# Expert weights loaded during the mixing stage, and the whole down product as rounded products, with ScalarE copying the result

## What is computed

```
x    = x + gt1 * rms_norm(mixed, g_post_mix)
hn2  = rms_norm(x, g_pre_ffn) * (1 + sc2) + sh2
group  = argmax(hn2 @ w_group_router + b_g)             # 4 groups
top 2 of the 4 experts of that group, weights from two softmaxes
act  = silu(hn2 @ w_gate[e]) * (hn2 @ w_up[e]) * weight # 16 experts, width 256
ffn  = sum over the two experts of act @ w_down[e]
x    = x + gt2 * rms_norm(ffn, g_post_ffn)
```

## Time and profile before

| | |
|---|---|
| median of three runs | 1550.93 us |
| the profiled execution, its own time | 1550.65 us |
| its span in the trace | 1548.8 us |
| TensorE busy | 1337.6 us, 86% |
| VectorE busy | 1140.9 us, 74% |
| ScalarE busy | 752.1 us, 49% |
| mixing ends, experts begin | at about 957 and 959 us of the span |
| loop: gate_up(2) begins, last down ends | at 1027 and 1481 us |
| bytes moved in the slice from 968 to 1007 us | 351 GB/s |

### The profile page before, as it was taken

The page is one execution under the profiler, slowest core; times in us unless marked ns, Lnnn a source line. Parts: engine busy times, 40 slices in busy tenths (PEclk is TensorE's granted clock), DMA queues, the critical chain, the costliest instruction groups (busy, mean ns, idle before and its releaser), DMA issues. The chain is left out here.

```text
span 1548.8 us, 24582 instructions
## 1 busy us (share of the span) xinstructions
PE 1337.6 (86%) x7046; PEld 1016.0 (66%) x7047; DVE 1140.9 (74%) x2094; ACT 752.1 (49%) x1614; POOL 538.8 (35%) x720
## 2 busy tenths in 40 slices
PE   5999999989997798699999994489999999999910
PEld 2688888856665465577777773267777777777700
DVE  3888888747675776366666664788989988988738
ACT  2423323213337477244444441167777777777633
POOL 1116776632226820012221122234443544444300
PEclk9999999979999999799999997699999999999965
DMA  9423444499867541333334433946798887884597
GB/s 335 131 94 133 180 157 156 153 341 342 291 209 209 165 138 58 132 136 136 135 135 161 157 129 127 351 133 158 195 267 239 252 240 191 267 222 107 129 327 287
DMA packets 138558, 298.30 MB, mean 193 GB/s; under 512 B 22228, under 2 KB 79829, under 8 KB 135998
## 3 DMA queue, kind: packets, MB, share of 16 engines
q1 hardware_dynamic: 110950, 219.74, 40.9%
q0 software_dynamic: 20800, 61.13, 17.0%
q10 hardware_dynamic: 6736, 16.55, 3.0%
HBM read 314.69 MB, written 102.25 MB: 269 GB/s over the span
## 5 line engine op out<-in xcount | busy, mean ns | idle before, releaser
L2683 DVE TENSOR_TENSOR ex_w_lo<-ex_wgu,ex_w_hi 128x1024 fp32r<-128x1024 f32 x192 | 226.1, 1220 | 47.6 <-ACT ex_w_hi L2480 46.9
L2480 ACT ACTIVATE ex_w_hi<-ex_wgu 128x1024 fp32r (+1 forms) x192 | 192.3, 1055 | 44.3 <-issue 31.0
L2443 POOL DMA_INDIRECT scratch_acc<-ex_o,ex_to x48 | 95.7, 1994 | 251.5 <-DVE ex_o L2713 170.7
L120 PE MATMUL ex_ps_h<-ex_w_hi,ex_xT 128*128 128x512 f32 x384 | 156.2, 407 | 3.4 <-DVE ex_x_lo L2677 3.4
L122 PE MATMUL ex_ps_h<-ex_w_hi,ex_x_lo 128*128 128x512 f32 x384 | 151.8, 395 | 0.0
L121 PE MATMUL ex_ps_h<-ex_w_lo,ex_xT 128*128 128x512 f32 x384 | 151.1, 393 | 0.0
L120 PE MATMUL fr_ps_m<-fr_whi,fr_hl 128*128 128x512 f32 (+1 forms) x384 | 138.7, 361 | 0.9 <-DVE fr_wlo L631 0.5
L122 PE MATMUL fr_ps_m<-fr_whi,fr_hl 128*128 128x512 f32 (+1 forms) x384 | 136.0, 354 | 0.0
L121 PE MATMUL fr_ps_m<-fr_wlo,fr_hl 128*128 128x512 f32 (+1 forms) x384 | 135.9, 354 | 0.0
L1941 POOL TENSOR_SCALAR mx_st<-mx_st 128x1 f32<-128x1 f32 x68 | 29.4, 433 | 268.1 <-ACT mx_j L1985 151.5
L120 PE MATMUL mx_ps_m<-mw_hi,mx_hT 128*128 128x512 f32 x272 | 107.9, 397 | 4.1 <-issue 2.1
(11 more groups left out here) (479 smaller groups left out, 3378.9 us busy)
## 6 DMA issues: line engine op xcount, KB each, us to landing
ex_wgu<-in_w_exp_gate_dram SPq DMA_DIRECT2D x51, 1024.0 KB, 11.8
ex_wgu<-in_w_exp_up_dram SPq DMA_DIRECT2D x51, 1024.0 KB, 14.1
ex_wd<-in_w_exp_down_dram SPq DMA_DIRECT2D x51, 1024.0 KB, 13.6
scratch_rec<-fr_w SPq DMA_DIRECT2D x16, 1112.0 KB, 4.2
s_rec<-scratch_rec SPq DMA_DIRECT2D x32, 556.0 KB, 5.8
scratch_proj<-fr_io SPq DMA_DIRECT2D x16, 640.0 KB, 3.0
scratch_acc<-in_zeros_dram SPq DMA_DIRECT2D x18, 512.0 KB, 5.7
scratch_x<-mx_x SPq DMA_DIRECT2D x17, 512.0 KB, 2.7
```

The costliest lines, as they stand in the source:

```text
L120: nc.tensor.matmul(out, hi, w_hi, start=first, stop=False)
L2443: pool.indirect_dma_start(T["acc"], bass.IndirectOffsetOnAxis(to[:, t:t + 1], 0), o[:, t % 2, :], None, compute_op=ALU.add).then_inc(sem(" ...
L2480: A(w_hi[:, par, c * PW:(c + 1) * PW], wgu[:, bass.ds(slot * (KD * 2 * DE) + c * PW, PW)], ACT.Copy).then_inc(S["w_rounded"], 1)
L2683: vec.tensor_tensor(w_lo[:, par, c * PW:(c + 1) * PW], wgu[:, bass.ds(slot * (KD * 2 * DE) + c * PW, PW)], w_hi[:, par, c * PW:(c + 1) * P ...
```

## The change

1. A new class `Routing` holds buffers that lie where the mixing weights lay. SP loads the constants at the start of mixing, and as soon as the last output product is done (`mix_done`) it issues the six loads of the first experts' gate and up weights, inside mixing. Tile 16's two stores go to ScalarE's queue. `square_mix` of tile 16 moves ahead of `move` of tile 15.
2. At the entry of `moe` the waits for the constants go. SP issues `w5` at once. TensorE's product with it comes before the sort products. VectorE takes the first part of `split_w(0)` ahead of `cmp`, the rest and the modulation row later. SP counts up the semaphores of the first three tiles itself, so ScalarE's `round_w(1)` and `round_w(2)` wait for the plan and the loads and not for SP.
3. AHEAD becomes 3: SP's order is `gate_up_weights(t+3)`, then `down_weights(t)`.
4. The second 128 rows of the down product become three rounded products too. `round_d` and `split_d` do both halves of the weights and of `a`. VectorE's `out` goes; ScalarE copies both halves of the result. TensorE's register reads go.
5. NKEPT becomes 1, so 16 tiles of `x2` are loaded at the end instead of 14.

```diff
+    def load_first(self, sp, T):
+        slots = self.wgu[:, :].rearrange("p (s k f) -> p s k f", s=NSL, k=KD)
+        for e in range(NSL):
+            for half, name in enumerate(("w_exp_gate", "w_exp_up")):
+                view = T[name].rearrange("a e (k p) f -> p (a e) k f", p=P)
+                sp.dma_start(slots[:, e, :, half * DE:(half + 1) * DE], view[:, e, :, :]).then_inc(self.first_gu[e], 16)
...
-            store(Tile(0, LAST))
-            sp.wait_ge(S["kept"], 32)
+            sp.wait_ge(S["mix_done"], NT)
+            plan.load_first(sp, T)
+            sp.wait_ge(S["kept"], 64)
...
                 if after:
                     glu(after)
+                else:
+                    square_mix(tile)
...
-            square_mix(Tile(0, LAST))
             square_x2(Tile(0, LAST))
+            end = Tile(0, LAST)
+            act.wait_ge(S["hn_ready"], NT)
+            act.dma_start(hnv[:, LAST:LAST + 1, :], hn[:, end.par, :].unsqueeze(1)).then_inc(end.sem("sth"), 16)
+            act.dma_start(x2v[:, LAST:LAST + 1, :], x[:, end.par, :].unsqueeze(1)).then_inc(end.sem("stx"), 16)
...
-NKEPT = 3
+NKEPT = 1
 LAG = 3
-AHEAD = 2
+AHEAD = NSL
...
+            for n in range(NSL):
+                sp.sem_inc(S["gu", n], 32)
+                sp.sem_inc(S["d", n], 16)
...
-            for t in range(AHEAD):
-                gate_up_weights(t, t)
+            for t in range(U):
+                gate_up_weights(t + AHEAD, (t + AHEAD) % U)
+                if t >= NSL:
+                    down_weights(t, t)
+            store_row5()
...
-            with sp.Fori(0, NTILE // U - 1) as i:
+            with sp.Fori(1, NTILE // U - 1) as i:
                 for n in range(U):
                     gate_up_weights(i * U + n + AHEAD, (n + AHEAD) % U)
                     down_weights(i * U + n, n)
...
-                A(a_hi[:, :], ps_a[:, 0:P], ACT.Copy, scale=0.5).then_inc(S["a_moved"], 1)
-                A(aT[:, 1, :], ps_a[:, P:2 * P], ACT.Copy, scale=0.5).then_inc(S["a_moved"], 1)
+                A(a_hi[:, :, :], ps_a[:, 0:2 * P].rearrange("p (k n) -> p k n", k=2), ACT.Copy, scale=0.5).then_inc(S["a_moved"], 1)
...
-                A(wd_hi[:, :], wd[:, bass.ds(slot * (2 * D), D)], ACT.Copy).then_inc(S["d_rounded"], 1)
+                for k in range(2):
+                    A(wd_hi[:, k, :], wd[:, bass.ds(slot * (2 * D) + k * D, D)], ACT.Copy).then_inc(S["d_rounded"], 1)
...
-                A(o[:, par, 0:512], ps_o[:, 0:512], ACT.Copy).then_inc(S["o_out_a"], 1)
+                for c in range(2):
+                    A(o[:, par, c * 512:(c + 1) * 512], ps_o[:, c * 512:(c + 1) * 512], ACT.Copy).then_inc(S["o_out_a"], 1)
...
-                vec.tensor_tensor(wd_lo[:, :], wd[:, bass.ds(slot * (2 * D), D)], wd_hi[:, :].bitcast(F32), ALU.subtract).then_inc(S["d_split"], 1)
+                for k in range(2):
+                    dve.wait_ge(S["d_rounded"], t * 2 + k + 1)
+                    vec.tensor_tensor(wd_lo[:, k, :], wd[:, bass.ds(slot * (2 * D) + k * D, D)], wd_hi[:, k, :].bitcast(F32), ALU.subtract).then_inc(S["d_split"], 1)
...
-                    three_products(nc, ps_o[:, at], a_hi[:, :], a_lo[:, :], wd_hi[:, at], wd_lo[:, at], True, False)
-                    last = nc.tensor.matmul(ps_o[:, at], aT[:, 1, :], wd[:, bass.ds((slot * 2 + 1) * D + c * 512, 512)], start=False, stop=True)
+                    pe.wait_ge(S["o_out_a"], t * 2 + c + 1)
+                    for k in range(2):
+                        last = three_products(nc, ps_o[:, at], a_hi[:, k, :], a_lo[:, k, :], wd_hi[:, k, at], wd_lo[:, k, at], k == 0, k == 1)
```

More of the change, by code:

```diff
@@ L1804, with mixing @@
 GELU_C = 2.0 * math.sqrt(2.0 / math.pi) / 2.0
-def mixing(nc, T, top, m, lg):
+def mixing(nc, T, top, m, lg, plan):
     with Stage(nc, top, "mx") as s:
@@ L1915, in _ @@
             clear(NT)
+            sp.dma_start(plan.rc[:, :], T["rconst"]).then_inc(S["kept"], 16)
+            sp.dma_start(plan.before[:, :], T["before"]).then_inc(S["kept"], 16)
             for b in range(2):
@@ L2651, in _, with split_w @@
                 dve.wait_ge(S["matched"], n + 1)
+            def split_w(t, par, parts, slot):
+                for c in parts:
+                    dve.wait_ge(S["w_rounded"], t * PARTS + c + 1)
+                    vec.tensor_tensor(w_lo[:, par, c * PW:(c + 1) * PW], wgu[:, bass.ds(slot * (KD * 2 * DE) + c * PW, PW)],
+                                      w_hi[:, par, c * PW:(c + 1) * PW].bitcast(F32), ALU.subtract).then_inc(S["w_split"], 1)
+            split_w(0, 0, range(1), 0)
             tt(cmp[:, :, :], C["tau"][0:1, :].unsqueeze(2).broadcast_to([1, NTILE, NE]), end[0:1, :].unsqueeze(1).broadcast_to([1, NTILE, NE]), ALU.is_ge)
@@ L2728, in step @@
                     split_w(t + 2, par, range(PARTS // 2), slot)
-                out(t - 1, 1 - par, i * (U // 2) + (k - 1) // 2)
                 split_d(t, own)
@@ L2769, in _ @@
             nc.tensor.matmul(ps_c, ones_h[:, :], a16, start=True, stop=True).then_inc(S["counted"], 1)
+            pe.wait_ge(S["w5_in"], 3 * 16)
+            for k in range(KD):
+                for j in range(4):
+                    last = nc.tensor.matmul(ps_h[32 * j:32 * j + 32, 1, 0:256], c5[:, k, :], w5(k)[:, j * 256:(j + 1) * 256], start=(k == 0), stop=(k == KD - 1))
+            last.then_inc(S["mm5"], 1)
             for n in range(2):
@@ L2774, in _ @@
             last.then_inc(S["turned"], 1)
-            pe.wait_ge(S["w5_in"], 3 * 16)
-            for k in range(KD):
-                for j in range(4):
-                    last = nc.tensor.matmul(ps_h[32 * j:32 * j + 32, 0, 0:256], c5[:, k, :], w5(k)[:, j * 256:(j + 1) * 256], start=(k == 0), stop=(k == KD - 1))
-            last.then_inc(S["mm5"], 1)
             def flip_x(t, n, q, first=False):
@@ L2867, in hybrid_layer @@
     early = Semaphores(nc)
-    with Stage(nc, None, "kept") as kept:
+    with Semaphores(nc) as top, Stage(nc, None, "kept") as kept, Stage(nc, top, "route") as route:
         lg = kept.sb("lg", [P, NT, NR])
@@ L2876, in hybrid_layer @@
             with Stage(nc, late, "mw") as weights:
-                mw = MixingWeights(weights)
+                plan = Routing(route)
+                mw = MixingWeights(weights, plan)
                 attention(nc, T, late, mw, first, early)
-                mixing(nc, T, late, mw, lg)
-        with Semaphores(nc) as top:
-            moe(nc, T, top, lg)
+                plan.constants(route)
+                mixing(nc, T, late, mw, lg, plan)
+        moe(nc, T, top, lg, plan)
 INS = ["x_prompt", "x_sample", "cache_k", "cache_v", "state_ssm_re", "state_ssm_im", "c_prompt", "c_sample",
```

144 lines of the change are left out of this document (68 added, 76 removed).

## The result

| | before | after |
|---|---|---|
| median of six runs beside each other | 1552.03 us (1549.96 to 1556.07) | 1557.85 us (1555.91 to 1559.91) |
| profiled execution, its own time | 1550.65 us | 1556.37 us |
| span of that execution | 1548.8 us | 1554.5 us |
| last logits of the mixing stage | 957.20 us | 952.05 us |
| `flip_x(3)` to the last `flip_x`, 44 periods | 426.94 us | 439.28 us |

The ratio is 1.0031, with a 95% interval of 1.0017 to 1.0045. The changed kernel is slower, by 5 to 6 us: more than the measurement is uncertain, less than the 0.5% that the forecast took as its bound for a difference. The forecast was 1550.

What follows compares the result with a forecast made beforehand. TensorE, busy 420 of 420 us, bounds the loop, VectorE close behind; nothing is full at the entry. 1550.65 - 9.9 (entry) + 6.5 (loop: -15.5 + 15 + 7) + 2.5 (end) = 1549.75, forecast 1550, range 1536 to 1564.

Steps and rivals of the forecast that it cites:

- TensorE's share: Loop: three rounded matmuls replace the float32 pair, saving 0.35 us a tile, 15.5 us in 44, if TensorE never waits.
- The register read: Loop: ScalarE's slow read before `round_w`, formerly hidden by slack, now comes through in part: +15 us, between 11 and 22.
- Rival (a): Loop: the engines keep up, reads hidden and down loads in time, TensorE sets 9.35: 1528 us, chance 0.12.
- AHEAD and the down weights: Loop: down loads behind fresh pairs land 1 to 2.5 us late in six tiles: +7 us, bounds 0 to 15.
- Rival (c): Loop: the clock falls in the stalls of the six late loads, 14 us on top: 1564 us, chance 0.13.
- The entry: From tile 16's `square_mix` to `gate_up(2)`: earlier work and fewer waits give -9.9 us, bounds -6 and -12.
- The barrier: Entry: SP, blocked issuing six megabytes until about 956.5, holds the barrier 1.5 us past the logits: +1.5 us.
- The end: After the loop: two more loads of 0.5 MB stand before the last scatter: +2.5 us, between 0 and 3.
- Kept at nothing: Semaphores, the constants' early loads in mixing and TensorE's dropped reads were given no cost or gain.
- (b): Loop: only one cost bites; reads without late loads 1543 us, loads without reads 1536 to 1541; chance 0.18.
- (d): Loads land at 17 us or more, or the entry gives only 6: +8 to +10, 1558 to 1562 us, chance 0.15.
- a period of 9.35: Loop, a sign of being right: TensorE's period without waits falls from 9.7 to 9.35 us.

Runs made afterwards that it cites:

- e5: Kernel of e1 with the old down product put back (second half one full float32 product, VectorE and ScalarE sharing the result copy): 1548.62 us, ratio 0.9980.
- e1: Changed kernel with each step issuing the down weights of tile t+1, not t, behind the gate and up weights of tile t+3: 1539.52 us, ratio 0.9921.
- e4: Kernel of e1 with GpSimd's next gather moved ahead of its three small operations, those one tile further on: 1537.88 us, ratio 0.9904.
- e3: Kernel before with only its constant AHEAD at 3 in place of 2: 1564.52 us, ratio 1.0084.
- e10: Kernel of e1 with 4 MB, not 6, of early expert weights, the third pair following the modulation weights after the barrier: 1543.66 us, ratio 0.9944.
- e8: Kernel of e1 with GpSimd's scatter of each tile also waiting for the next tile's second rounded down weights: 1549.24 us, ratio 0.9994.
- e7: Kernel of e1 with the places of `ex_w_hi` and `ex_w_lo` in memory exchanged: 1539.04 us, ratio 0.9915.

## Why the prediction was wrong

The loop was forecast at +6.5 us and was +12.3, from two large errors of opposite sign and a smaller one: the reads came out 14.5 us below their term, the late loads 14.2 above theirs, TensorE's gain some 6 short. That the measured time still lies within the stated range of 1536 to 1564 is luck: the two large errors cancel. No change was forecast, and the kernel became slower.

- **TensorE's share, -15.5.** Right in its mechanism. Measured by e5 against e1, 0.31 us a tile and not 0.35: -13.6. What failed beside it is a term that the sum doesn't have: the new places in memory make `gate_up` 0.10 longer, +4.5 in 44 tiles (e5's loop against that of before). The prediction went through the diff's new buffers for room and order, never for the speed of the reads from them.
- **The register read, +15.** Wrong, the largest error. It is 0.5 us in the changed kernel. The step that failed is that the read would stay as in the earlier trace rows: I costed the read as a property of the instruction's place beside the gather, and held its length fixed while the change moved what makes it long. The prediction even says that the scatters start 2 us earlier, as a relief for the loads, but doesn't ask what else that relieves. The other half of the step was right: a read that is long in a tile without a late load has no cover in the new chain (e1's seven, 3.8 us in all), where the old one hid 28 of them. In the changed kernel six of the seven long reads stood in the shadow of the late loads. Rival (a) had the outcome with the wrong cause; e4 excludes the gather.
- **AHEAD and the down weights, +7.** Right tiles, right number (six), right mechanism; the size was a third of the 21.2 measured, and outside the bounds of 0 to 15. Tile 10 shows where. The load landed 19 us after P(t-1), not 17, 17.0 us after the pair's first issue; `round_d` wanted it at 14.8 us, not 15.4; so it is late by 4.2, not 1 to 2.5. Why it lands 2 us later than worked out is not shown. I had taken the lower end of my own bound because scatters move away; nothing supported that. And the wait then goes through whole.
- **Rival (c), the clock.** It exists, at a fifth of its price. The pauses of 2.72 and 2.50 us were followed by matmuls at the lower clock, and these two down products took 4.43 and 4.21 us, not 2.88: 2.9 us in all, within the 21.2. After the pause of 1.81 us, and the three shorter ones, the clock stayed up. The prediction let the length of the pause decide, from a point between 2.0 and 5.5 us. The traces don't bear that out: 2.26 us in e3 (before 1292.70) left the clock up, and of the same pause of 2.01 us in mixing the kernel before came out with the clock up and the changed kernel with it down. What else decides is not shown. The stretches after pauses of 2.72 and 1.81 us in the changed kernel, of 2.26 in e3, and of 2.01 in mixing, changed and before (stretch; us; TensorE busy; granted clock, where 1.00 is 2.4 GHz and 0.50 is 1.2; DMA):

```profile
1112.24:1115.50 3.26, 3.26 (x8) 0.52 0.56 161
1252.80:1255.80 3.00, 2.98 (x12) 1.00 0.62 152
...
1292.70:1295.90 3.20, 3.20 (x11) 1.00 0.97 257
...
924.20:927.80 3.60, 3.60 (x9) 0.56 0.02 5
...
928.40:932.00 3.60, 3.58 (x16) 1.00 0.02 5
```

- **The entry, -9.9.** -7.2, within its bounds. By its own steps: `square_mix` gave -2.5 of -2.4, the constants' wait its -2.6, `gate_up(0)` to `gate_up(1)` -4.3 of -4.4, and from there to `gate_up(2)` -1.3, not -0.7. The barrier is the step that failed: +3.7 (2.39 us after the last logits became 6.12), not +1.5. I had SyncE blocked in issuing until 956.5. It was done at 950.4, and waited then for a store of tile 16 that ScalarE's queue had issued at 947.18 and that landed some 8 us later, beside 6 MB of weights:

```profile
947.18 0.45 ACTq L2077 DMA_DIRECT2D scratch_x<-mx_x  x1
...
946.23 4.20 SPq L123 DMA_DIRECT2D route_wgu<-in_w_exp_up_dram  x1
...
SPq L1961 <- DMA scratch_x<-mx_x: 4.9, 1, 4.9
```

  e10 supports in part that these weights delay the store: a third less of early loads, 1.5 us less of wait. The first gather was 0.3 us quicker, not 1, and the first transposes took 1.94 us, not 1.07, which ate the gain of VectorE's emptier start. `gate_up(2)` began at 1017.42, the forecast's 1017.4, but only because mixing was 2.6 us early.
- **The end, +2.5.** +3.1, right in size, but not where it was looked for. The last scatter did not move back against the last `down`: it starts 3.4 us after its end, 4.7 before. The 3.1 us lie between that scatter and the first load of `acc` (5.9 us before, 9.1 after). From the last `flip_x` to that load the three kernels with 14 loads of `x2` take 32.1 to 32.8 us and those with 16 take 33.5 to 35.1, so the two loads go with 0.7 to 3 us; how they delay it is not shown.
- **Kept at nothing**: the product with `w5`, rightly; it was done 1.2 us before VectorE had the next input for TensorE ready. Nor does a wait for the semaphores or the constants show.
- **Rivals (b) and (d).** What happened is the second half of (b), late loads without the reads, which by the prediction's own terms is 1535 (it says 1536 to 1541). It came out at 1557.85, mainly as the late loads cost 21.2 and not 7, the new places in memory 4.5, and the barrier 2.2 more than allowed. That this is the number of (d), 1558 to 1562, is luck as well: the loads did land later than 17 us, as (d) has it, but (d) keeps the 15 us of reads.

What was named as a sign in the prediction: scatters earlier (2.5 us in the median), down weights waited for in six tiles, matmuls 0.43 apart inside the loop, `gate_up(2)` at 1017.4: seen. A last scatter 2 us later against the last `down` (it is 1.3 earlier), a period of 9.35, some 20 us of waits of `gate_up` for `ex_x_lo` (3.6), VectorE over 93% busy (92.4%): not seen. The changed kernel is slower through one constant, which makes the down loads late: with the down load put back where it was (e1) the same change is 12 us faster than the kernel before, 18 faster than as it stands.

## What to carry to other kernels

When a load is given more lead, look at what shares its queue: a constant that issues one stream earlier issues the next one later, and the price is read by laying the landing time of the late one beside the time at which it is wanted, at the new period and without the waits that the change takes away. A wait whose cause isn't known can't be carried over at its old size; ask first what it goes with (here, the time since the last scatter), and whether the change moves that. And where an engine's share is forecast to 0.05 us a tile, the places of the operands in memory belong to the change as well.

## What the runs showed of the hardware

- A read of one word from on-chip memory into a sequencer's register mostly takes 0.26 to 0.32 us (medians in the changed kernel: SyncE 0.27, ScalarE 0.28, VectorE 0.31), and over all kernels one in seven takes more than 0.5, up to 1.8. ScalarE's long ones began 2.5 to 4.2 us after the start of GpSimd's indirect scatter with accumulation in the kernels before and after, e1, e4 and e8; in e7 and e10 three of 22 began outside that. VectorE's reads are long too (26 of 88 in e1, up to 1.6 us). The Trainium skill (DMA: Bandwidth & Descriptors, Latency and other measured facts) has a floor of about 600 ns for such loads; over half of those in these traces are under 0.3.
- The same 24 matmuls take 5.58, 5.60 or 5.69 us in the median, each within 0.04 in a kernel's loop, by where their operands lie in memory (e7 against e1: two buffers exchanged, nothing else).
- Pauses of TensorE: after 1.81 and 2.26 us the next stretch had a granted clock of 1.00, after 2.72 us one of 0.52; after 2.01 us it was 1.00 in one kernel and 0.56 in another.
